# Gated linear attention: weights prepared by halves among the chunks, scores in row tiles of one head each

## The reference, cut to what matters

```
S_t = diag(f_t) S_{t-1} + k_t v_t^T ;  o_t = S_t^T q_t
# chunkwise, cum = cumulative sum of log f inside a chunk:
scores[i,j] = sum_d q[i,d] * exp(cum[i,d] - cum[j,d]) * k[j,d]     (j <= i)
out   = scores @ v + (q * exp(cum)) @ S
S     = exp(cum[last]) * S + (k * exp(cum[last] - cum))^T @ v
```

## Time and profile before

| | |
|---|---|
| median of 3 runs | 3340.0 us (3337.72 to 3342.39) |
| the profiled execution, its own time | 3340.4 us |
| its span, first to last instruction | 3338.8 us |
| mean granted TensorE clock | 0.937 of full speed |
| busy: TensorE, VectorE, ScalarE, GpSimd | 2937.0, 1674.2, 979.9, 706.7 us |
| gated linear attention, in the span | 330.2 to 570 us |

### The profile page before, as it was taken

One profiled execution on the slowest core, in us unless ns is written; L12 is line 12 of the kernel. 1 busy time (PEld: TensorE's weight loads), 2 busy tenths in 40 slices (PEclk: granted clock), 3 DMA queues, 4 the chain that ended last, 5 costly groups with the idle time before them and its releaser, 6 DMA issues. The chain is left out here.

```text
span 3338.8 us, 38597 instructions
## 1 busy us (share of the span) xinstructions
PE 2937.0 (88%) x14688; PEld 2323.1 (70%) x14688; DVE 1674.2 (50%) x2776; ACT 979.9 (29%) x1870; POOL 706.7 (21%) x445
## 2 busy tenths in 40 slices
PE   6999456878999999969999799988899998999988
PEld 4767346336888888857768687766677676877766
DVE  4170876223323313232478763476534787634865
ACT  3151221111001001020268342175103673421751
POOL 1233000002333333214111301402141113014021
PEclk8999678888999999989999899999999998999989
DMA  3011001101111121113112001203231120012032
GB/s 106 33 32 38 0 1 50 55 6 67 35 58 51 35 67 45 35 66 105 27 38 76 26 1 51 70 8 126 89 107 26 43 75 23 1 52 73 4 126 89
DMA packets 78797, 168.35 MB, mean 50 GB/s; under 512 B 14848, under 2 KB 33808, under 8 KB 78096
## 3 DMA queue, kind: packets, MB, share of 16 engines
q1 hardware_dynamic: 70160, 140.61, 12.6%
q10 hardware_dynamic: 8448, 25.18, 2.7%
HBM read 128.00 MB, written 20.97 MB: 45 GB/s over the span
## 5 line engine op out<-in xcount | busy, mean ns | idle before, releaser
L296 PE MATMUL psum<-H,ffn_W 128*128 128x512 f32 x672 | 262.8, 391 | 12.8 <-POOL ffn_W L1278 11.1
L297 PE MATMUL psum<-H,ffn_W 128*128 128x512 f32 x672 | 262.3, 390 | 0.0
L298 PE MATMUL psum<-H,ffn_W 128*128 128x512 f32 x672 | 262.2, 390 | 0.0
L1276 POOL CAST ffn_W<-ffn_W 128x1024 fp32r<-128x1024 f32 (+1 forms) x84 | 69.4, 826 | 680.8 <-PE psum L298 447.2
L290 PE MATMUL psum<-CONST 128*128 128x512 f32 x116 | 74.4, 799 | 134.2 <-ACT XT_mixer L1017 77.5
L1573 DVE TENSOR_SCALAR_CACHE_REDUCE MB<-OM,tk_mid 128x512 bf16<-128x512 f32 (+2 forms) x192 | 184.3, 1010 | 2.3
L1352 DVE TENSOR_SCALAR ffn_Y<-ffn_G,ffn_par 128x1024 f32<-128x1024 f32 x21 | 22.1, 1052 | 297.5 <-ACT ffn_G L1341 297.5
L1542 ACT ACTIVATE MB<-OM,tk_mid 128x384 bf16<-128x384 f32 (+2 forms) x192 | 157.0, 819 | 48.5 <-DVE tk_mid L1570 44.4
L482 POOL TENSOR_TENSOR tk_W<-tk_W 128x1024 fp32r<-128x1024 f32 (+1 forms) x38 | 78.7, 2074 | 424.7 <-ACT tk_W L434 424.7
L1278 POOL TENSOR_TENSOR ffn_W<-ffn_W 128x1024 fp32r<-128x1024 f32 (+1 forms) x84 | 161.7, 1925 | 6.7
L296 PEld LDWEIGHTS psum<-H,ffn_W 128*128 128x128 f32 x672 | 126.7, 188 | 40.3 <-POOL ffn_W L1278 11.5
(11 more groups left out here) (417 smaller groups left out, 7502.8 us busy)
## 6 DMA issues: line engine op xcount, KB each, us to landing
OM<-in_w_feat SPq DMA_DIRECT2D x34, 512.0 KB, 4.3
tk_W<-in_w_feat SPq DMA_DIRECT2D x22, 512.0 KB, 3.5
ffn_W<-in_ffn_w_gate SPq DMA_DIRECT2D x21, 512.0 KB, 3.4
ffn_W<-in_ffn_w_val SPq DMA_DIRECT2D x21, 512.0 KB, 3.5
ffn_W<-in_ffn_w_down SPq DMA_DIRECT2D x42, 256.0 KB, 2.7
OM<-MB ACTq DMA_DIRECT2D x64, 128.0 KB, 2.6
OM<-OM ACTq DMA_DIRECT2D x64, 128.0 KB, 3.0
fin_W<-in_w_out SPq DMA_DIRECT2D x4, 2048.0 KB, 10.6
```

Of the source, the lines that this page charges most:

```text
L296: pe.matmul(out, a1, b1, start=start, stop=False)
L297: pe.matmul(out, a1, b2, start=False, stop=False)
L298: return pe.matmul(out, a2, b1, start=False, stop=stop)
L1276: pool.tensor_copy(w1, w).then_inc(rounded, 1)
```

## The change

The stage computes the same. Three things are different.

1. A tile is prepared by halves of four chunks (512 columns), six halves `u` in all. Each half is cut in three parts. Half 0 is prepared ahead of the loop; every other part stands in VectorE's and ScalarE's program behind the state update, or the output copy, of one chunk (`prep_at`): chunks 0, 1, 2 of passes 0, 1, 2 carry the second half of their own tile, chunks 4, 5, 6 of passes 0 and 1 the first half of the next tile. That is 15 of the 32 steps. TensorE transposes the keys of a half (`keys`) in chunks 3 and 7, behind a wait for `mixed`, the end of the third part.
2. Scores are made one head at a time, with that head's 64 or 32 rows of KW and QW alone, each head into a PSUM bank of its own. QW has no zeros and no place for a second head: one instruction weighs 128 partitions for both heads (and, in tile 2, for both passes), so pass 3 needs no new QW and GpSimd clears nothing.
3. The masks are read as integers where they lie, with no conversion; Z has four places of half the width; the state is cleared by halves at the start of a pass; there is one spin, ahead of the first keys, of four products (eight passes) where each tile had two.

`levels_of(part)` gives levels (0, 1), (2, 3) and (4, 5, 6). The first `prep_at` hunk is the rule, the second stands in VectorE's program, the one with `out_done` in ScalarE's.

```diff
+    def prep_at(p, c):
+        if c < 3:
+            return (2 * tile_of[p] + 1, c) if p == 0 or tile_of[p - 1] != tile_of[p] else None
+        if CH <= c < CH + 3:
+            return (2 * tile_of[p + 1], c - CH) if p + 1 < NP and tile_of[p + 1] != tile_of[p] else None
+        return None
...
-                for n, p in enumerate((0, 2, 3)):
-                    if p:
-                        pool.wait_ge(out_done, NT * p)
-                    stale = slice(0, 64) if p == 3 else slice(0, P)
-                    pool.memset(flat[stale, 0:NL * S], 0.0).then_inc(cleared, 1)
...
-                own(dve.tensor_copy(LM[:, :], level))
-                own(dve.tensor_copy(DM[:, :], ident))
                 own(dve.memset(SC, 0.0))
+                own(dve.memset(ST, 0.0))
...
+                def weigh(u, n):
+                    g, b = u // 2, LEVELS[n]
+                    dve.wait_ge(weights, N_Z * u + (n if n < TAIL else n + 1) + 1)
+                    own(dve.tensor_tensor(QW[:, n, CH * (u % 2):CH * (u % 2 + 1), :]
+                                          .rearrange("p c (m w) -> p c m w", w=b),
+                                          w4[:, :, :, b:2 * b], q4[:, :, :, b:2 * b], ALU.mult))
+                    own(dve.tensor_tensor(w3, w3, k3, ALU.mult))
+
+                def prep(u, part):
+                    g = u // 2
+                    if part == 0:
+                        if freed(u):
+                            dve.wait_ge(out_done, freed(u))
+                        own.then(dve.tensor_tensor_scan(half_of(C, u), half_of(keep, u), half_of(LF[:, g, :], u), 0.0,
+                                                        ALU.mult, ALU.add))
                         dve.sem_inc(cums, 1)
+                        for seq in (0, 1, 2):
+                            refer(u, seq)
+                    elif part == 1:
+                        for seq in (3, 4):
+                            refer(u, seq)
                     else:
+                        for seq in (6, 7):
+                            refer(u, seq)
+                    for n in levels_of(part):
+                        weigh(u, n)
+                    if part == 1:
+                        own(dve.tensor_tensor(half_of(QK, u), half_of(Q[:, g, :], u), half_of(K[:, g, :], u), ALU.mult))
+                        refer(u, TAIL)
+                    elif part == 2:
+                        own(dve.tensor_tensor(half_of(QE, u), half_of(QE, u), half_of(Q[:, g, :], u), ALU.mult))
+                        own(dve.tensor_tensor(half_of(KL, u), half_of(KL, u), half_of(K[:, g, :], u), ALU.mult))
                         own.wait()
                         dve.sem_inc(mixed, 1)
...
+                        if prep_at(p, c):
+                            prep(*prep_at(p, c))
...
                     for c in range(NT):
-                        act.wait_ge(out_done, NT * p + c + 1)
+                        step = NT * p + c
+                        act.wait_ge(out_done, step + 1)
                         act.activation(O[:, c, P * p:P * (p + 1)], kit.psum[:, 6, 0:P], ACT.Copy
                                        ).then_inc(out_taken, 1)
+                        if prep_at(p, c):
+                            prep(*prep_at(p, c))
...
                     for n in range(NL):
-                        pe.matmul(bank[:, n * P:(n + 1) * P], KW[:, n, at],
-                                  QW[:, n, c, :, :].rearrange("p h m -> p (h m)"), start=True, stop=True)
-                    pe.matmul(bank[:, NL * P:NL * P + 2], QK[:, at], heads[:, 2 * p:2 * p + 2],
-                              start=True, stop=True).then_inc(scored, 1)
+                        for h, r in enumerate(rows_in[p]):
+                            pe.matmul(kit.psum[:, 2 * (step % 2) + h, n * 64:(n + 1) * 64], KW[r, n, at],
+                                      QW[r, n, c, :], start=True, stop=True)
+                    for h, r in enumerate(rows_in[p]):
+                        last = pe.matmul(kit.psum[:, 2 * (step % 2) + h, NL * 64:NL * 64 + 1], QK[r, at],
+                                         heads[r, 2 * p + h:2 * p + h + 1], start=True, stop=True)
+                    last.then_inc(scored, 1)
+
+                def keys(u):
+                    pe.wait_ge(mixed, u + 1)
+                    if u >= 2:
+                        pe.wait_ge(kt_taken, u - 1)
...
+                pe.wait_ge(weights, NL)
+                spin(kit, pe, 3, 4)
+                keys(0)
+                scores(0, 0)
...
+                        if c == CH - 1 and p < 3:
+                            keys(2 * tile_of[p] + 1)
+                        if c == NT - 1 and p < 2:
+                            keys(2 * tile_of[p + 1])
+                        if step + 1 < NT * NP:
+                            scores(*divmod(step + 1, NT))
```

More of the change, by code:

```diff
@@ L868, in gla_stage, with freed, levels_of @@
     NP = len(PASS_ROWS)
[L869 to L873, removed]
+    CH = NT // 2
+    TAIL = 5
+    N_Z = NL + 1
+    cums, refs, weights, mixed, kept, kt_done, kt_taken, scored, placed, out_done, out_taken, \
+        upd_done, upd_taken, own_d, state_set = (
+            kit.sem(f"gla_{n}") for n in ("cums", "refs", "weights", "mixed", "kept", "kt_done", "kt_taken", "scored",
+                                          "placed", "out_done", "out_taken", "upd_done", "upd_taken", "own_d",
+                                          "state_set"))
     tile_of = [0, 1, 2, 2]
+    pass_of = [0, 1, 2]
     flat = X.rearrange("p t n -> p (t n)")
+    rows_in = [[slice(first + h * dk, first + (h + 1) * dk) for h in range(2)] for first, dk in PASS_ROWS]
+    def prep_at(p, c):
[4 more added lines that the diff above has]
+        return None
+    def freed(u):
+        p, half = pass_of[u // 2], u % 2
+        return NT * (p - 1) + CH * (half + 1) if p else 0
+    def levels_of(part):
+        return ((0, 1), (2, 3), (4, 5, 6))[part]
     with ExitStack() as mem:
@@ L967, in _ @@
+                for part in range(3):
+                    prep(0, part)
+                for p in range(NP):
+                    rows = rows_in[p]
+                    if p:
+                        dve.wait_ge(out_done, NT * p - 1)
+                        own.then(dve.memset(ST[:, 0, :], 0.0))
                     dve.sem_inc(state_set, 1)
@@ new lines, in prep, with keys_turned @@
+                def prep(u, part):
+                    if part == 0:
+                        act.wait_ge(cums, u + 1)
+                    for seq in ((0, 1, 2), (3, 4, TAIL), (6, 7))[part]:
+                        bend(u, seq)
+                def keys_turned(u):
+                    act.wait_ge(kt_done, u + 1)
+                    act.activation(half_of(KLT, u), kit.psum[:, 4 + u % 2, :], ACT.Copy).then_inc(kt_taken, 1)
+                for part in range(3):
+                    prep(0, part)
@@ new lines, in scores @@
+                    for h, r in enumerate(rows_in[p]):
[6 more added lines that the diff above has]
+                        pe.wait_ge(kt_taken, u - 1)
+                    for n in range(CH):
+                        m = CH * (u % 2) + n
+                        last = pe.transpose(kit.psum[:, 4 + u % 2, n * P:(n + 1) * P], KL[:, m * P:(m + 1) * P], ident)
+                    last.then_inc(kt_done, 1)
```

193 lines of the change are left out of this document (73 added, 120 removed).

## The result

| | before, same chip | after |
|---|---|---|
| median | 3341.1 us (13 runs, 3336.9 to 3346.6) | 3349.4 us (13 runs, 3344.4 to 3356.5) |
| ratio | 1 | 1.0025, 95% interval 1.0016 to 1.0034 |
| profiled execution, its span | 3340.4, 3338.8 us | 3347.5, 3345.8 us |
| mean granted clock | 0.937 | 0.920 |
| end of the stage in the span | 570 | 576.5 (forecast 530.6) |

The change made the kernel 8 us slower; 3301 was forecast. Behind the stage nothing moved: 3345.8 less 576.5 is 2769.3 us, and it was 2768.8.

The account below looks back on a forecast made before the run. VectorE (preparations) and TensorE (loops) bound the stage in turn. 110 + 23.5 + 44.2 + 1.2 = 179 us replaces 199.7, gaining 20.7; with 18.6 ahead, 39.3 off 3340.4 gives 3301 us, range 3287 to 3331.

Parts of the forecast that it names:

- The step becomes 3.48 + 0.2 = 3.7: Row-tile step set by TensorE: old period 3.48 us plus two switches between tiled and full products, 0.2, if pairs overlap.
- For twelve steps ... 44.2: Last four steps of pass 2 and eight of pass 3, at 3.7 us each: 44.2 us.
- the mixed steps: Fifteen steps carrying a third of a half preparation, bound by VectorE: 7.3 us each, 110 us in all.
- Both fit under 7.3: In mixed steps, TensorE's 3.7 us at the upper clock and 7.0 at the lower hide under VectorE's 7.3.
- Case B: VectorE's parts dearer or lower clock sticking: a half 14.5 us, five boundary steps 6.3 each; about 3317 us, 18%.
- The start: Without mask conversions the scan starts at 332.0, not 337.55; first place at 351.7, not 370.3: gain 18.6 us.
- The half preparation: VectorE's preparation of 512 columns: differences 0.61 us apart, weighings 0.34, 13.0 us in all, between 12.5 and 14.5.
- The boundary: Chunks 3 and 7, TensorE waiting for `mixed`: 4.7 us a step, between 3.0 and 6.3; five steps, 23.5 us.
- The overlap of pairs: In row-tile scores, two row groups load and multiply together at one full pass's price, about 0.11 us.
- case C: Passes of the two heads run one after the other: twelve row-tile steps at 5.5 us; 3332 us, 14%.
- case D: Passes follow one another and each pays its load openly, 0.192 us; steps 8.0 us, 3382 us, slower than before, 6%.
- case E: Clock stays up through mixed steps (boundaries 3.0 us, -8.5), a half at 12.5, shorter spin: 3287 us, 6%.

Follow-up runs that it names:

- filled and doubled: Changed kernel with unread full-height products in TensorE's pauses in the mixed part and each row-tile score's query columns read twice: 3300.5 us, ratio 0.9869.
- one product more: Last kernel of the experiments: filled and doubled, with four unread products in place of three at the boundary into pass 2: 3294.6 us, ratio 0.9855.
- the run of row tiles alone: Kernel before, its order of work kept, with scores in row tiles, QW without zeros and no clearing: 3391.3 us, ratio 1.0151.
- the streams from 0.50: Two kernels: the one before with unread product streams in its three preparations, begun at the lower clock: 3398.8 and 3371.8 us, one execution each.

## Why the prediction was wrong

**The step that failed** is "The step becomes 3.48 + 0.2 = 3.7", "For twelve steps ... 44.2", as a length at 2.4 GHz. The steps took 6.57 at 1.2 GHz: 31.7 of the 46 us by which the stage ended late. I took for granted that a TensorE without pauses is at the upper clock, as in the earlier trace rows. That the same edit which cuts a product's rows and width might also keep the clock down was in no case. The price at the lower clock was at hand: the prediction gives 7.0 for it in the mixed steps, and used it for none of the twelve. Where the clock was held, with the columns doubled, a step was 3.76.

**The second step** is "Both fit under 7.3". It compared TensorE's length at the lower clock (7.0) with VectorE's and took the chain scores, place, L1137, output copy, exponentials to cost little. The four steps behind a boundary took 10.9 each, with 3.0 us of waiting for ScalarE in them, and the other eleven 7.5 in place of 7.3: together the +16.1. Case B had both "the lower clock sticking" and, in its 6.3 a boundary, ScalarE late by 1.3, but priced them at the five boundaries only. With the measured 2.9 more for each of the twelve row-tile steps, 34, the forecast would have been 3335, and with the mixed steps 3351.

**What came as forecast.** The start (350.4 for 351.7); its masks alone gave 5.1 us. The half preparation: differences 0.60 apart, weighings 0.33; and at the upper clock, in the last kernel of the experiments, the fifteen mixed steps take 110.1 for 110. The boundary, 4.6 for 4.7, and 2.7 to 2.9 at the upper clock for 3.0. The overlap of pairs: 28 passes in 1.78, so case C and case D are out, and so is the rule of the Trainium skill, "TensorE: Matmul & The Clock Gate", Part 3, as far as it would have put 5.5 us on a step. (Case C's terms add up to 3331, its upper end in the range; the 3332 in its line is a slip of one.) The switch between tiled and full products: 3.76 a step with the doubled columns, 3.48 + 0.2 + 0.05 = 3.73.

**What the runs leave together.** With the clock held in the last twelve steps, the kernel takes 3300.5, and held all through the stage 3294.6, the forecast being 3301. The agreement of the first is in part luck. The terms of the two kernels, from the starts of L996:

| term | forecast | filled and doubled | one product more |
|---|---|---|---|
| first place | 351.7 | 351.9 | 351.8 |
| fifteen mixed steps | 110 | 117.0 | 110.1 |
| five boundary steps | 23.5 | 14.0 | 13.9 |
| twelve row-tile steps, clearing | 45.4 | 44.7 | 44.7 |
| end of the stage | 530.6 | 527.5 | 520.5 |

In the first, two steps behind the boundary into pass 2 are dear (+7) and the boundaries cheap (-9.5). In the second all terms are right but the boundaries, which were priced near the lower clock; this is what case E had for them (3.0 each). So the lengths were right at the clock that each was priced at; the sum was that of another kernel, one whose TensorE stays at 2.4 GHz in the last twelve steps.

The pause of 3.33 us preceded the fall, and the same products without a pause stayed at 1.00 for 14 us (the mix with 64-row pairs). That the products then kept the clock down is shown by the run of row tiles alone, where no pause follows, by the streams from 0.50, and by width alone bringing it back at times in passes 0 and 1. "TensorE: Matmul & The Clock Gate", Part 1, of the Trainium skill has the clock follow how busy TensorE has been; by that alone the stretch of 77.34 busy in 78.00 us should have been at 2.4 GHz, and the trace disagrees.

**Left open.** Whether the fall at the boundary into pass 2 needed both the pause of 1.16 us and the 32-row scores behind it: the kernel that avoids it changes the pause and adds a full product at once. In the same way the filled pauses take the pauses away and add full products, so no run tells which of the two kept passes 0 and 1 at 1.00. And the streams are six points, one execution each, not a law of rows and width.

## What to carry to other kernels

A product made smaller, in rows or in columns, can cost no less and still take the clock down for everything around it: read the granted clock of the stretch, not only busy shares, and price every step at both levels over its whole stretch. Where a pass of 64 columns costs what one of 128 does, as here (0.05 us for 28 passes), columns are nearly free, and a repeated operand helped to keep the clock up; alone it did so in part (ratio 0.9994). Pauses made by interleaving another engine's work are worth filling with full products while the filled step still hides under that engine (1.0025 to 0.9968 here, 19 us; 57 together with the columns and one product more).

## What the runs showed of the hardware

- TensorE busy 77.34 of 78.00 us stayed at 1.2 GHz; so did unbroken streams of 38 us of full-height products of 64 columns, of 64-row pairs of 64 columns and of single 64-row products of 128 columns.
- In a stream of 64-row pairs of 128 columns the clock came back, as in one of full-height products of 128 columns (22.97 and 22.68 us for the same number of pair or full slots).
- 32-row pairs of 64 columns lost the upper clock without any gap, alone and in a step's mix; steps with 32-row pairs of 128 columns stayed at it for the last twelve steps, but did not come back to it in 31.00 busy us.
- Two fp32 passes of one head followed by two of the other overlap as well as heads in turn: 1.78 us for 28 passes, 3.25 at 1.2 GHz.
